# Twelve of sixteen v rows on VectorE in the jobs beside prompt attention

## The chip, the cores and the metric

The kernel runs on one core of one Trainium2 chip. The metric is the device time of one execution in microseconds (us); lower is better. The core has TensorE (PE, matrix products into PSUM), VectorE (DVE), ScalarE (ACT), GpSimd (POOL) and SyncE (SP). Here POOL only issues gathers, SP and ACT issue plain transfers. Each engine runs its own instructions in order and waits on semaphores for the others.

## The reference

One decoder layer for a prompt of 1024 tokens and 8 x 8 sample tokens: RMSNorm with modulation, one input projection into q, k, v, convolution inputs and gates, a short causal convolution, dilated window attention in three head groups, two gated output projections, and then PEER. PEER is what the change touches:

```python
q = (xb @ w_query)...                      # 8 heads, two halves of 128
s1, s2 = q halves @ sub_keys               # 128 scores each, top 16 of each
top_s, top_pos = top_k(v1[:, None] + v2[None, :], 16)
gate = softmax(top_s)
act  = einsum('td,thkd->thk', xb, expert_u[eidx])
coef = gate * gelu(act)
out  = einsum('thk,thkd->td', coef, expert_v[eidx])
```

For each token and head, 16 rows of `expert_u` are dotted with the token's row, and 16 rows of `expert_v` are added up with weights `coef`. Every row is 1024 floats.

## The kernel before

A tile is 128 tokens, and there are 9 of them (the third holds the 64 sample tokens). The first 0.76 ms prepare modulation, the first two tiles and the sample tokens. All else is in `peer`, one program on all engines at once.

**Jobs.** A job is one tile and one head; there are 72, numbered by tile and then head. Loop s (0 to 72) gathers the u rows of job s and the v rows of job s-1. POOL issues them in the order u(s, k), v(s-1, k) for k = 0 to 15. One gather fetches 128 rows, one for each token: 512 KB. The u rows land in a ring of 8 slots, the v rows in another ring of 8. So v row k + 8 can be gathered only once v row k has been used (line 1506 and on: POOL waits on `v_weighed` if TensorE uses row k, on `v_added` if VectorE does).

**The two ways to add a v row.** TensorE: ScalarE writes a diagonal matrix of the weights (line 2107), and `weigh` (line 1787) multiplies it with the row into PSUM. VectorE: `add_row` (line 2459) multiplies and adds the row into `acc`. `on_vector(s, k)` says which engine takes row k of job s. In jobs 0 to 47 VectorE takes the odd rows and TensorE the even ones; from job 48 on VectorE takes 5 rows.

**VectorE's loop.** For each k: a step of the ranking of a later job (`experts`), the dot of u row k (`dot`, line 2443), `add_row` where the v row is its own, then background. At the end of the loop `coefs` (lines 2466 to 2483) makes the weights; line 2483 ends the loop.

**Background.** Beside the jobs runs the front part of the layer for the next three tiles (segments): norm, input projection (line 1682 and others), attention, mixing (line 1700), output projection, queries. `chain_order` numbers its PSUM banks, 6 of which are used in turn. `limit(s, f)` turns the place in the jobs (loop s, fraction f) into the number of the last bank that the background may have reached. VectorE calls `pace.up_to(limit(s, k / 16))` behind every k. TensorE does this behind each of its v rows:

```python
for i, r in enumerate(rows):
    weigh(r)
    pace.up_to(limit(s, min(0.9, (i + 3) / len(rows))))
```

`rows` are TensorE's rows of job s-1. So the number of rows that TensorE has sets where its background goes between them.

**Attention of a segment.** It lies in loops 9 to 12 (first half of the table below) and 33 to 38. There are 12 items (head pair, tile, head) in each segment. For an item TensorE makes scores (mask line 1613, product line 1614) in 2 to 4 banks; VectorE takes their maximum (lines 2236 to 2242, the function `top`); ScalarE the exponentials (line 1948); TensorE transposes them (line 1650); ScalarE copies these to SBUF (line 1967); TensorE multiplies with v (line 1637). The scores of item i+1 stand before the transposes of item i on TensorE, and on ScalarE the exponentials of item i+1 stand before the copies of item i.

Of the kernel before, what the change touches and what calls it, by code (L numbers as in the profile page):

```python
# [1008 lines left out]

JOBS = NT * HEADS  # L1010
WINDOW = 48
LATE = 52
SEG = 3
SEGS_N = NT // SEG
# [10 lines left out]
def width(s):  # L1025
    return TOPK // 2 if s // HEADS == PS else TOPK


def rows_before(s):

    return TOPK * s - TOPK // 2 * min(max(s - PS * HEADS, 0), HEADS)
# [4 lines left out]


def on_vector(s, k):
    return k in ((1, 3, 5, 7, 9, 11, 13, 15) if s < WINDOW else (2, 5, 8, 11, 14))


def added_by():

    on_pe, on_dve = {}, {}
    for s in range(JOBS):
        for k in range(width(s)):
            mine = on_dve if on_vector(s, k) else on_pe
            mine[rows_before(s) + k] = len(mine)
    return on_pe, on_dve
# [131 lines left out]
def peer(nc, io, keep):  # L1181
    with ExitStack() as ctx:
# [161 lines left out]
        def wait_emptied(eng, key):  # L1344
            eng.wait_ge(emptied[number[key] % NB], number[key] // NB + 1)
# [468 lines left out]
        def _(act):  # L1814
# [267 lines left out]
            def raise_h2(t):  # L2082
                act.wait_ge(h2_in[t % 2], 16 * (t // 2 + 1))
                if t == LATE // HEADS:
                    for key in list(number)[-NB:]:
                        wait_emptied(act, key)
                if t > LATE // HEADS + 1:
                    act.wait_ge(u_used, rows_before(HEADS * (t - 1)))
                for c in range(2):
                    act.activation(psB[:, 2 * (t % 2) + c, :], h2[:, t % 2, c * 512:(c + 1) * 512],  # L2090
                                   ACT.Copy).then_inc(h2_raised, 1)
# [35 lines left out]
            for s in range(JOBS + 1):  # L2127
# [19 lines left out]
                if s < JOBS:  # L2147
                    act.wait_ge(gelu_in, s + 1)
                    act.activation(g4[:, 0:width(s)], g3[:, 0:width(s)], ACT.Exp, scale=-GELU).then_inc(gelu_exp, 1)  # L2149
                if s == LATE - 1:  # L2150
                    raise_h2(t)
                if h == 7 and LATE // HEADS < t + 1 < NT:
                    raise_h2(t + 1)
# [6 lines left out]
        def _(dve):  # L2160
# [274 lines left out]
            def dot(s, k):  # L2435
                t, r = s // HEADS, rows_before(s) + k
                if k == 0 and s % HEADS == 0:
                    dve.wait_ge(h2_in[t % 2], 16 * (t // 2 + 1))
                if s >= LATE and (s == LATE or s % HEADS == 0) and k == 0:
                    dve.wait_ge(h2_raised, 2 * (t - LATE // HEADS + 1))  # L2440
                dve.wait_ge(u_in[r % U], 16 * (r // U + 1))
# [80 lines left out]
            for s in range(JOBS + 1):  # L2522
                t, h = divmod(s, HEADS)
                if h == 1 and t:
                    finish(t - 1)
                for k in range(TOPK):
                    if k <= NAMED_AT:
                        next(choosing, None)
                    if k == NAMED_AT:
                        for _ in choosing:  # L2530
                            pass
                        choosing = experts(s + 2) if s + 2 < JOBS else iter(())
                    if TOPK - RANKED <= k:
                        next(choosing, None)
                    if s < JOBS and k < width(s):
                        dot(s, k)
                    if s and k < width(s - 1) and on_vector(s - 1, k):
                        add_row(s - 1, k)
                    pace.up_to(limit(s, k / TOPK))
                if s < JOBS:  # L2540
                    coefs(s)
                if h == 0 and t:
                    gather_up(t - 1)
# [81 lines left out]
```

## Time and profile before

| | |
|---|---|
| time, median of 3 runs | 4194.48 us (4192.9 to 4195.76) |
| profiled execution, its own time | 4189.91 us |
| its span in the profile | 4187.2 us |
| PE / DVE / POOL busy | 78% / 69% / 59% of the span |
| loops 9, 10, 11 (attention of the second segment) | 65, 71, 62 us |
| loops 34, 35, 36, 37 (attention of the third) | 55, 57, 60, 49 us |
| a loop beside other background, 13 | 50 us |

A loop is counted here from one end of `coefs` to the next. "Released by" in the profile names the instruction that ended a wait. POOL's busy time is the time in which it issues gathers; the landing comes later and is given by the view of a line.

### The profile page before, as it was taken

The numbers are of one execution on the slowest core, as the hardware profiler recorded it, in microseconds if no ns is written. First come the engines' busy times: TensorE is split into PE (matmuls) and PEld (weight loads), VectorE is DVE, ScalarE is ACT, GpSimd is POOL, SyncE is SP. The second block draws the span as 40 slices with busy tenths as digits, with TensorE's granted clock in tenths as the row PEclk, the third lists the DMA queues.
The fourth block names the chain that finished last, engine by engine and source line by source line (L and its number), as shares of the span: only waits on it lengthen the run. The fifth ranks groups of instructions, "written<-read, shape, count | busy, mean of one in ns | idle before, by whom it ended". The sixth has DMA issues, their size and how long they took to land. (4 is left out here: it accounts for less than half of the span.)

```text
span 4187.2 us, 33973 instructions
## 1 busy us (share of the span) xinstructions
PE 3280.6 (78%) x9782; PEld 1758.2 (42%) x9798; DVE 2895.2 (69%) x6507; ACT 635.6 (15%) x1759; POOL 2488.9 (59%) x2277
## 2 busy tenths in 40 slices
PE   6978898788888987788888888887777666566666
PEld 1445575654444544455444445444444222222222
DVE  2212111678786777988878987787778788778875
ACT  0020001221012212123110133111111111101010
POOL 0001000477764677567787666876777777777775
PEclk9968898899997899889998898998888888988888
DMA  7316344799997999999999989999999999999998
GB/s 257 124 34 174 98 121 150 277 403 403 393 387 255 331 387 396 352 391 376 401 402 390 385 320 335 390 391 387 387 393 391 373 409 409 408 409 397 405 409 323
DMA packets 578893, 1405.09 MB, mean 336 GB/s; under 512 B 44731, under 2 KB 276347, under 8 KB 578683
## 3 DMA queue, kind: packets, MB, share of 16 engines
q0 software_dynamic: 320080, 1165.57, 71.7%
q1 hardware_dynamic: 223070, 196.45, 15.0%
q10 hardware_dynamic: 35560, 40.91, 2.8%
q8 instruction: 81, 1.33, 0.1%
q14 instruction: 102, 0.84, 0.1%
HBM read 1369.31 MB, written 33.44 MB: 335 GB/s over the span
## 5 line engine op out<-in xcount | busy, mean ns | idle before, releaser
L1787 PE MATMUL peer_psA<-peer_vring,peer_diag 128*128 128x512 f32 x2464 | 1394.8, 706 | 626.4 <-DMA peer_vring<-in_expert_v,peer_idx 474.3
L1501 POOL DMA_INDIRECT peer_uring<-in_expert_u,peer_idx x1088 | 1224.4, 1125 | 713.6 <-DVE peer_idx L2416 360.7
L1511 POOL DMA_INDIRECT peer_vring<-in_expert_v,peer_idx x1088 | 1222.4, 1124 | 548.2 <-issue 301.0
L2443 DVE CUSTOM_DVE_ANT_0 peer_uring<-peer_uring,peer_h 128x1024 f32<-128x1024 f32 x768 | 934.6, 1217 | 218.7 <-DMA peer_uring<-in_expert_u,peer_idx 217.0
L1787 PEld LDWEIGHTS peer_psA<-peer_vring,peer_diag 128*128 128x128 f32 x2464 | 509.6, 221 | 1353.2 <-issue 1165.3
L2459 DVE SCALAR_TENSOR_TENSOR peer_acc<-peer_vring,peer_coef,peer_acc 128x1024 f32<-128x1024 f32 x463 | 593.9, 1283 | 86.2 <-DMA peer_vring<-in_expert_v,peer_idx 80.7
L2443 DVE CUSTOM_DVE_ANT_0 peer_uring<-peer_uring,peer_psB 128x1024 f32<-128x1024 f32 x320 | 388.8, 1215 | 142.8 <-DMA peer_uring<-in_expert_u,peer_idx 142.5
L1682 PE MATMUL peer_psB<-keep_hT,peer_w 128*128 128x384 f32 (+1 forms) x864 | 279.2, 483 | 12.2 <-DMA peer_w<-in_w_in 12.2
L1756 PE MATMUL peer_psB<-peer_w,keep_hT 128*128 128x256 f32 x1152 | 273.4, 393 | 18.4 <-DMA peer_w<-in_w_query 17.3
L1700 PE MATMUL peer_psB<-keep_hT,peer_w 128*128 128x384 f32 (+1 forms) x768 | 250.8, 482 | 20.8 <-DMA peer_w<-in_w_attn_o 20.8
L1756 PEld LDWEIGHTS peer_psB<-peer_w,keep_hT 128*128 128x128 f32 x1152 | 228.5, 200 | 76.5 <-issue 28.2
L2149 ACT ACTIVATE peer_g<-peer_g 128x16 f32<-128x16 f32 (+1 forms) x72 | 15.5, 215 | 1459.7 <-DVE peer_g L2473 1459.7
L1682 PEld LDWEIGHTS peer_psB<-keep_hT,peer_w 128*128 128x128 f32 x864 | 170.4, 198 | 125.8 <-issue 23.9
L1700 PEld LDWEIGHTS peer_psB<-keep_hT,peer_w 128*128 128x128 f32 x768 | 150.4, 197 | 121.4 <-DMA peer_w<-in_w_attn_o 25.0
L2107 ACT ACTIVATE peer_diag<-keep_ident,peer_coef 128x128 f32<-128x128 f32 x616 | 187.8, 388 | 59.8 <-DVE peer_coef L2483 59.8
L1579 PE MATMUL peer_psB<-peer_w,keep_hT 128*128 128x384 f32 x576 | 196.4, 496 | 0.0
L1579 PEld LDWEIGHTS peer_psB<-peer_w,keep_hT 128*128 128x128 f32 x576 | 113.0, 197 | 88.1 <-issue 23.4
L1729 PE MATMUL peer_psB<-peer_w,peer_mT 128*128 128x384 f32 (+3 forms) x432 | 130.6, 461 | 3.0 <-DVE peer_mT L2325 3.0
L1637 PE MATMUL peer_psB<-peer_w,peer_arena 128*128 128x64 f32 x576 | 89.2, 314 | 37.7 <-ACT peer_arena L1967 37.7
L1614 PE MATMUL peer_psB<-peer_w,peer_mT 64*128 64x512 f32 (+3 forms) x224 | 104.9, 552 | 3.4 <-issue 1.8
L1637 PEld LDWEIGHTS peer_psB<-peer_w,peer_arena 128*128 128x128 f32 x576 | 86.3, 232 | 49.1 <-issue 44.6
L1729 PEld LDWEIGHTS peer_psB<-peer_w,peer_mT 128*128 128x128 f32 (+1 forms) x432 | 81.7, 190 | 56.1 <-issue 17.2
(245 smaller groups left out, 2943.8 us busy)
## 6 DMA issues: line engine op xcount, KB each, us to landing
peer_w<-in_w_in SPq DMA_DIRECT2D x102, 512.0 KB, 21.8
peer_w<-in_w_query SPq DMA_DIRECT2D x24, 1024.0 KB, 15.7
peer_w<-in_w_in SPq DMA_DIRECT2D x12, 1536.0 KB, 18.4
peer_uring<-in_expert_u,peer_idx POOLq DMA_INDIRECT x1088, 10.7
peer_vring<-in_expert_v,peer_idx POOLq DMA_INDIRECT x1088, 10.6
front_ring<-in_w_ada POOLq DMA_DIRECT2D x7, 2048.0 KB, 8.3
front_ring<-in_w_ada SPq DMA_DIRECT2D x5, 2048.0 KB, 7.8
peer_w<-in_w_conv_o SPq DMA_DIRECT2D x24, 384.0 KB, 23.1
```

What stands on the lines that cost most here:

```text
L1501: pool.indirect_dma_start(out=uring[:, r % U, :], out_offset=None, in_=io["expert_u"], in_offset=bass.IndirectOffsetOnAxis(ap=idx[:, s % 4 ...
L1511: pool.indirect_dma_start(out=vring[:, r % V, :], out_offset=None, in_=io["expert_v"], in_offset=bass.IndirectOffsetOnAxis(ap=idx[:, s % 4 ...
L1579: last = pe.matmul(dst[:, 0:WQKV], hT[:, k, i * P:(i + 1) * P], wv[:, k, :], start=(k == 0), stop=(k == DC - 1))
L1637: last = pe.matmul(bank(key_o)[:, 0:HD], pT[:, t_slot[g, it, b] % 2, (at % 4) * P:(at % 4 + 1) * P], vv[:, kb, col:col + HD], start=(at == ...
L1682: last = pe.matmul(dst[:, 0:m], wv[:, k, part, :], hT[:, k, 0:m], start=(k == 0), stop=(k == DC - 1))
L1700: last = pe.matmul(dst[:, 0:m], wv[:, KC_AT[q] + k, :], src[:, k, 0:m], start=(k == 0), stop=(k == KC[q] - 1))
L1729: last = pe.matmul(dst[0:R, 0:e - a], mT[:, k, i * P:i * P + R], wv[:, k, :], start=(k == 0), stop=(k == DC - 1))
L1756: last = pe.matmul(dst[:, 0:KD], hT[:, k, j * P:(j + 1) * P], wv[:, k, :], start=(k == 0), stop=(k == DC - 1))
L1787: last = pe.matmul(psA[:, c * 512:(c + 1) * 512], diag[:, a % DG, :], vring[:, r % V, c * 512:(c + 1) * 512], start=first, stop=False, ski ...
L2107: act.activation(diag[:, a % DG, :], ident[:], ACT.Copy, scale=coef[:, s % 4, k:k + 1]).then_inc(diag_set, 1)
L2443: dve.tensor_tensor_reduce(uring[:, r % U, :], uring[:, r % U, :], rows, 1.0, 0.0, ALU.mult, ALU.add, act_[:, k:k + 1]).then_inc(u_used, 1)
L2459: dve.scalar_tensor_tensor(out=acc[:], in0=vring[:, r % V, :], scalar=c, in1=acc[:], op0=ALU.mult, op1=ALU.add).then_inc(v_added, 1)
```

## The change

In jobs 8 to 13 and 32 to 37 VectorE takes 12 of the 16 v rows, and TensorE rows 0, 4, 8 and 12. Their rows are added in loops 9 to 14 and 33 to 38. The counts behind the waits (`on_pe`, `on_dve`) follow from `on_vector`. 48 rows go from TensorE to VectorE; ScalarE writes 48 diagonals fewer.

```diff
+ATTENDING = ((8, 14), (32, 38))
 LATE = 52
...
 def on_vector(s, k):
+    if any(a <= s < b for a, b in ATTENDING):
+        return k not in (0, 4, 8, 12)
     return k in ((1, 3, 5, 7, 9, 11, 13, 15) if s < WINDOW else (2, 5, 8, 11, 14))
```

Line numbers behind it grow by 3. On TensorE, this is what stood in loop 10 from the scores of the seventh item on (psB: the 6 banks; psA: the sum of v rows; the weigh in the middle is v row 6 of job 9, the last one row 8; the program counts 2 products for a weigh, the trace 4):

```order
L1613 MATMUL peer_psB<-keep_mask,keep_identb 128x384
L1614 MATMUL peer_psB<-peer_w,peer_mT 128x384
L1613 MATMUL peer_psB<-keep_mask,keep_identb 128x128
L1614 MATMUL peer_psB<-peer_w,peer_mT 128x128
L1787 MATMUL peer_psA<-peer_vring,peer_diag 128x512 x2
L1613 MATMUL peer_psB<-keep_mask,keep_identb 128x256
L1614 MATMUL peer_psB<-peer_w,peer_mT 128x256
L1613 MATMUL peer_psB<-keep_mask,keep_identb 128x256
L1614 MATMUL peer_psB<-peer_w,peer_mT 128x256
L1650 MATMUL peer_psB<-keep_ident,peer_arena 128x128 x8
L1787 MATMUL peer_psA<-peer_vring,peer_diag 128x512 x2
```

And now at the same place of the same loop:

```order
L1616 MATMUL peer_psB<-keep_mask,keep_identb 128x384
L1617 MATMUL peer_psB<-peer_w,peer_mT 128x384
L1616 MATMUL peer_psB<-keep_mask,keep_identb 128x128
L1617 MATMUL peer_psB<-peer_w,peer_mT 128x128
L1616 MATMUL peer_psB<-keep_mask,keep_identb 128x256
L1617 MATMUL peer_psB<-peer_w,peer_mT 128x256
L1616 MATMUL peer_psB<-keep_mask,keep_identb 128x256
L1617 MATMUL peer_psB<-peer_w,peer_mT 128x256
L1653 MATMUL peer_psB<-keep_ident,peer_arena 128x128 x8
L1790 MATMUL peer_psA<-peer_vring,peer_diag 128x512 x2
```

The weigh between the scores is gone, and the one at the end is now v row 4. Between v row 0 and v row 4 stands all background up to three quarters of the loop (three items, 41 rows of the program) where three weighs stood between. Rows 8 and 12 follow together at 0.9.

On VectorE, rows k = 10 and 11 of the same loop before (dot, add of a v row, ranking, then the maximum of the seventh item's scores):

```order
L2443 ISA peer_uring,peer_act<-peer_uring,peer_h 128x1024
L2443 ISA peer_act 128x1
L2377 TENSOR_TENSOR peer_eq<-peer_v 128x256
L2443 ISA peer_uring,peer_act<-peer_uring,peer_h 128x1024
L2443 ISA peer_act 128x1
L2459 SCALAR_TENSOR_TENSOR peer_acc<-peer_vring,peer_coef,peer_acc 128x1024
L2236 TENSOR_REDUCE peer_mx<-peer_psB 128x1 x2
```

And now:

```order
L2446 ISA peer_uring,peer_act<-peer_uring,peer_h 128x1024
L2446 ISA peer_act 128x1
L2462 SCALAR_TENSOR_TENSOR peer_acc<-peer_vring,peer_coef,peer_acc 128x1024
L2380 TENSOR_TENSOR peer_eq<-peer_v 128x256
L2446 ISA peer_uring,peer_act<-peer_uring,peer_h 128x1024
L2446 ISA peer_act 128x1
L2462 SCALAR_TENSOR_TENSOR peer_acc<-peer_vring,peer_coef,peer_acc 128x1024
L2239 TENSOR_REDUCE peer_mx<-peer_psB 128x1 x2
```

One add more stands behind the dot of k = 10; the maximum stays behind k = 11.

## Rows read from the trace of the kernel before

**Rows 1.** The page's head: the span.

```profile
span 4187.2 us, 33973 instructions
```

**Rows 2.** The page's costliest groups: out<-in, count | busy, mean ns | idle before.

```profile
L1787 PE MATMUL peer_psA<-peer_vring,peer_diag 128*128 128x512 f32 x2464 | 1394.8, 706 | 626.4 <-DMA peer_vring<-in_expert_v,peer_idx 474.3
L2459 DVE SCALAR_TENSOR_TENSOR peer_acc<-peer_vring,peer_coef,peer_acc 128x1024 f32<-128x1024 f32 x463 | 593.9, 1283 | 86.2 <-DMA peer_vring<-in_expert_v,peer_idx 80.7
```

**Rows 3.** Windows of loops: length, PE, PEld, DVE, ACT, POOL busy, granted clock, DMA, GB/s.

```profile
1222.00:1287.00 65.00, 56.87 (x178) 29.53 (x179) 52.21 (x120) 15.47 (x41) 37.19 (x35) 0.89 0.88 319
1287.00:1358.00 71.00, 64.95 (x219) 36.85 (x220) 46.12 (x107) 20.31 (x61) 32.06 (x29) 0.69 0.72 255
1358.00:1420.00 62.00, 53.33 (x195) 29.10 (x198) 47.53 (x115) 18.98 (x58) 35.37 (x33) 0.83 0.80 291
...
1469.00:1519.00 50.00, 43.31 (x114) 22.28 (x113) 41.02 (x92) 7.14 (x17) 40.08 (x33) 0.93 1.05 389
...
2328.00:2382.00 54.00, 45.69 (x125) 22.68 (x124) 49.91 (x113) 7.46 (x17) 35.50 (x33) 0.95 1.04 396
2382.00:2437.00 55.00, 49.04 (x159) 26.91 (x162) 45.89 (x108) 19.17 (x60) 29.88 (x28) 0.74 0.84 318
2437.00:2494.00 57.00, 50.99 (x213) 29.84 (x215) 46.08 (x109) 18.08 (x54) 35.29 (x35) 0.91 0.87 313
2494.00:2554.00 60.00, 50.87 (x198) 30.12 (x200) 45.67 (x104) 14.53 (x44) 38.46 (x35) 0.86 0.97 349
2554.00:2603.00 49.00, 41.33 (x197) 26.05 (x200) 43.20 (x102) 19.69 (x57) 32.54 (x29) 0.90 0.90 323
```

**Rows 4.** Waits in loops 9 to 11: us in total, times, longest.

```profile
POOL peer_vring L1511 <- PE peer_psA L1787: 66.2, 13, 17.1
DVE peer_mx L2236 <- PE peer_psB L1614: 45.3, 24, 5.9
```

**Rows 5.** Waits in loops 34 to 37.

```profile
POOL peer_vring L1511 <- PE peer_psA L1787: 51.5, 16, 14.0
...
DVE peer_mx L2236 <- PE peer_psB L1614: 29.0, 21, 5.4
```

**Rows 6.** TensorE in loop 10: start us, length us, engine, line, op [idle before].

```profile
1295.95 2.07 PE L1614 MATMUL peer_psB<-peer_w,peer_mT 64*128 64x512 f32 x2 [0.36 <-issue]
...
1312.74 0.63 PE L1613 MATMUL peer_psB<-keep_mask,keep_identb 128*128 128x512 bf16 x1
...
1315.31 3.42 PE L1787 MATMUL peer_psA<-peer_vring,peer_diag 128*128 128x512 f32 x4
...
1322.53 1.88 PE L1787 MATMUL peer_psA<-peer_vring,peer_diag 128*128 128x512 f32 x4
...
1330.33 0.53 PE L1613 MATMUL peer_psB<-keep_mask,keep_identb 128*128 128x384 bf16 x1
...
1341.61 3.62 PE L1787 MATMUL peer_psA<-peer_vring,peer_diag 128*128 128x512 f32 x4
```

**Rows 7.** Windows by clock in loop 10, columns as in the windows above.

```profile
1294.30:1318.20 23.90, 21.24 (x58) 12.13 (x59) 15.29 (x36) 4.30 (x12) 6.11 (x6) 0.50 0.54 199
1318.20:1328.50 10.30, 8.79 (x47) 5.32 (x44) 6.99 (x19) 4.04 (x11) 6.96 (x7) 1.00 0.72 234
```

**Rows 8.** VectorE at the end of loop 10: dot of row 13, last of `coefs`.

```profile
1343.72 1.22 DVE L2443 CUSTOM_DVE_ANT_0 peer_uring<-peer_uring,peer_h 128x1024 f32<-128x1024 f32 x1
...
1358.05 0.17 DVE L2483 TENSOR_TENSOR peer_coef<-peer_g,peer_gates 128x16 f32<-128x16 f32 x1
```

**Rows 9.** POOL in loop 10: v row 10, the next u row.

```profile
1319.00 0.94 POOL L1511 DMA_INDIRECT peer_vring<-in_expert_v,peer_idx  x1 [17.05 <-PE peer_psA L1787]
1320.24 0.94 POOL L1501 DMA_INDIRECT peer_uring<-in_expert_u,peer_idx  x1 [0.30 <-issue]
```

**Rows 10.** The line of the u gathers in loops 9 to 11: landing.

```profile
DMA to landing us min/median/max: 5.1/7.3/13.5
```

## The prediction

> **What bounds the kernel now.** I read the head of the page first, for the span [rows 1], then its groups, for what one add costs on either engine [rows 2], then windows cut at the ends of the loops that the change touches [rows 3], then who waits for whom in them [rows 4, 5], and last TensorE, VectorE and POOL in one of these loops, in order of time [rows 6 to 10].
>
> Beside other background a loop is bound by the gathers. In loop 13 the DMA engines are busy throughout (share 1.05) while TensorE has work for 43.3 of 50 us and VectorE for 41.0 [rows 3]. In the seven loops beside attention (9 to 11 and 34 to 37) the DMA share is 0.72 to 0.97, the loops are mostly longer, and something else is the bound: VectorE waits for scores, 45.3 us in three loops and 29.0 us in four, and POOL waits 66.2 and 51.5 us until TensorE has used a v row and freed its slot [rows 4, 5]. So there the engines go round an item together: scores, maximum, exponentials, transposes, products. TensorE holds the largest part of that round, 65.0 of 71 us in loop 10 [rows 3].
>
> VectorE and TensorE pass three quarters of the background of such a loop at about the same time as VectorE passes three quarters of its rows. In loop 10 TensorE reaches that mark at 1341.61, where it weighs v row 8 [rows 6], and VectorE dots u row 13 at 1343.72 [rows 8]. I call it the mark.
>
> **The change part by part.**
>
> *Weighs taken off TensorE.* One takes four products of 706 ns, 1394.8 / 616 = 2.26 us with its overlap [rows 2]; 48 make 108.7 us. Four leave each loop, and three of them (rows 2, 4 and 6, with row 4's now standing where row 8's stood) lie ahead of the mark. At most 3 x 2.26 = 6.8 us a loop, 7 x 6.8 = 47 us in the seven loops, comes off the round. In the other five loops it is worth nothing, since gathers or VectorE end last there.
>
> The lower bound comes from the items of loop 10. From the first scores of one item to those of the next it took 16.8 us (1295.95 to 1312.74) with no weigh in it; 17.6 (to 1330.33) with two weighs of 3.42 and 1.88 us; 18.0 us (to 1348.35, 9 further rows of the same pattern) with two more at about 3.6 us [rows 6]. Two weighs cost an item only about 1 us. The reason is in the clock: the granted share was 0.50, that is 1.2 GHz, from 1294.3 to 1318.2, and 1.00, that is 2.4 GHz, for the 10.3 us from there on [rows 7]. It rose as the weigh at 1315.31 was ending. TensorE was busy for 21.24 of the 23.9 us at the low level, most of it with scores, transposes and products with v, and none of that had brought the clock up. So a weigh in this stage pays for itself by the clock that follows. By this row three weighs fewer give a loop 1.5 to 2 us, 7 x 2 = 14 us in all; loops 35 to 37, now at 0.86 to 0.91 [rows 3], could even lose. I take 30 us, the middle of 14 and 47, since five of the seven loops run nearer to 2.4 GHz than loop 10 does.
>
> The Trainium skill (TensorE: Matmul & The Clock Gate, part 1, "What's actually happening") says that the low clock is the default and that activity of the engine releases it. By that rule alone the long busy stretch at 0.50 should have ended by itself, the clock would stay as it is now, and this term would be the full 47 us; the trace has it end at a weigh, so the row decides against the rule's plain form.
>
> *The gathers run dry.* This is what the change adds without a line for it. POOL gathers v row k + 8 only when row k is used, and u row k + 9 is behind that in its queue. Now TensorE's row k is weighed when the background stands at (k + 4) / 16 of the loop, and row k + 8 is needed at (k + 8) / 16: four rows ahead. The new rows 0, 4, 8, 12 are weighed at 0, 0.75, 0.9 and 0.9. So v row 12 can be asked for only behind the mark, when VectorE is at its own row 12, and u row 13 comes behind it. From the mark to the dot of row 13 this takes a weigh (2.26), POOL's start (0.27 behind the weigh, 1315.31 + 3.42 to 1319.00 [rows 6, 9]), one gather to the next (1.24), and the landing (5.1 at least, 7.3 in the middle [rows 10]): 8.9 to 11.1 us. Now it takes 2.1 us. The delay is 9.0 us by the middle landing. VectorE's three added adds ahead of the mark (3 x 1.283 = 3.8 us [rows 2]) partly fill it, so 5.2 to 9.0 us a loop; where VectorE is late for other reasons, nothing. I take 6, nearer to the lower, since a queue that has drained lands faster than the middle: 7 x 6 = 42 us.
>
> POOL's long waits now do no harm, because four rows of u lie in the ring meanwhile: the 17.05 us wait in loop 10 [rows 9] stands beside a VectorE that waits for scores and not for a row.
>
> *Adds put on VectorE.* 48 x 1.283 = 61.6 us [rows 2], 5.1 us a loop. Ahead of the mark the wait for scores hides them (45.3 / 3 = 15.1 and 29.0 / 4 = 7.3 us a loop [rows 4, 5]). Behind it stands one more add, v row 14, with only row 13's landing before it: 1.28 us a loop, 9 us in seven. Loop 33 has VectorE busy for 49.9 of 54 us [rows 3], and attention begins only in its last fifth; there the 5.1 us have 1 to 4 us of cover at most. I take 4 of 5.1. In loops 12, 13, 14 and 38 the gathers end last, VectorE has some 9 us to spare, as in loop 13 [rows 3], and I take 0, with 5.1 each, 20 us, as the other bound.
>
> *Diagonals off ScalarE.* 48 fewer, off the path; 0, between a gain of 0.4 us a loop and nothing.
>
> Sum: -30 + 42 + 9 + 4 = +25 us. The profiled execution took 4189.91 us, 2.7 us more than its span [rows 1]; the median of the runs is 4194.48, 4.6 us above it. The changed kernel comes to 4189.9 + 25 = 4215 us in such an execution, 4219.5 as a median.
>
> **The rivals.**
>
> *A, VectorE absorbs the work (faster).* TensorE's clock stays as it is, the round shortens by the whole 47 us, and VectorE, later by its added adds, finds row 13 landed. Then each loop lasts as long as VectorE's work. The seven loops have 326.7 us of it now; with 7 x 5.1 added, 7 us of small waits and 4 us a loop of landing they come to 398 against 419 us [rows 3]: 21 us less, and 4 us back in loop 33. Some 17 us faster, 4177 us. For it: the waits of VectorE for scores are real slack. Against it: it holds only if the delay behind the mark stays under 4 us in each loop, and no row shows that much room there.
>
> *B, the terms cancel (same).* The weighs give 47 us and the delay is 5 us a loop: -47 + 35 + 9 + 4 = +1, 4196 us.
>
> *C, nothing hides the adds (slower still).* VectorE becomes the bound in all twelve loops, because its rows 1, 2 and 3 now follow one another and each waits for its own landing: 61.6 us on top, 4256 us. Against it: loop 13's spare time, and the DMA share of 0.72 to 0.97 in the others.
>
> *D, the clock stays at 1.2 GHz between the marks.* The weighs give 14 us and the delay is 9 us a loop: -14 + 63 + 9 + 4 = +62, 4256 us as well. It is the forecast at its upper end.
>
> **How the numbers follow.** The forecast, between +9 and +50 us, gets 0.48, C and D together 0.15, B 0.17, A 0.20. A change of less than 0.2%, 8.4 us, can't be told from none here. Faster than that is A alone, 0.20; within it B, 0.17; slower the rest, 0.63. The likeliest case alone spans 4203 to 4245. The range that should hold the time 8 times in 10 takes in A's price and most of C and D: 4176 to 4252.
>
> **What would show it.** Right: one long wait of POOL for TensorE in each of the seven loops, at v row 12, instead of several; VectorE's wait for u rows in these loops at 4 us or more each, just behind the dot of row 12; its wait for scores shorter; the granted clock in loops 11 and 35 to 37 below 0.83 and 0.86; loop 33 longer by about 4 us; loops 12 to 14 and 38 unchanged. Wrong: the seven windows shorter than 419 us in all, with no wait for u rows; or a clock that rises between the marks without a weigh.

## The result and the profile after

The changed kernel takes 4281.39 us (median of 4 runs, 4279.10 to 4286.09), the kernel before, beside it, 4195.12 us (4192.90 to 4204.19). The ratio is 1.0208, with a 95% interval of 1.0194 to 1.0221: 86 us slower. The forecast was slower by 25 us, with a range up to 4252. The direction was right; the size lies outside the range. Of all executions in this document one stands apart, 6895.11 us among the six of e11_pace_five_eighths; its times and ratio below leave that one out.

The page of the changed kernel, head and the groups that answer to [rows 1, 2]. Lines stand 3 higher than before (weigh L1790, u gather L1504, v gather L1514, dot L2446, add L2462):

```profile
span 4279.6 us, 33590 instructions
...
L1790 PE MATMUL peer_psA<-peer_vring,peer_diag 128*128 128x512 f32 x2272 | 1311.2, 718 | 690.3 <-DMA peer_vring<-in_expert_v,peer_idx 489.5
...
L1514 POOL DMA_INDIRECT peer_vring<-in_expert_v,peer_idx x1088 | 1220.6, 1122 | 646.4 <-PE peer_psA L1790 321.9
L2446 DVE CUSTOM_DVE_ANT_0 peer_uring<-peer_uring,peer_h 128x1024 f32<-128x1024 f32 x768 | 934.5, 1217 | 293.9 <-DMA peer_uring<-in_expert_u,peer_idx 291.8
...
L2462 DVE SCALAR_TENSOR_TENSOR peer_acc<-peer_vring,peer_coef,peer_acc 128x1024 f32<-128x1024 f32 x511 | 655.4, 1283 | 87.7 <-DMA peer_vring<-in_expert_v,peer_idx 80.3
```

48 weighs (192 matmuls in the trace) have gone and 48 adds have come, at nearly the unit prices of before (718 and 706 ns for a weigh's product, 1283 for an add). The work did what the change says; the span grew by 92.4 us elsewhere. Windows cut at the ends of loops 9, 10, 11, 33 and 34 to 37, columns as in [rows 3]:

```profile
1224.00:1297.00 73.00, 52.07 (x163) 28.44 (x163) 57.70 (x125) 14.60 (x38) 30.90 (x30) 0.76 0.69 256
1297.00:1374.00 77.00, 60.71 (x203) 37.85 (x204) 51.29 (x115) 19.14 (x57) 35.55 (x34) 0.61 0.69 253
1374.00:1452.00 78.00, 57.59 (x183) 35.34 (x186) 51.92 (x115) 17.58 (x54) 34.54 (x35) 0.63 0.64 239
2359.00:2418.00 59.00, 41.55 (x110) 20.72 (x109) 54.91 (x117) 6.29 (x14) 33.37 (x32) 0.84 1.02 387
2418.00:2487.00 69.00, 52.57 (x158) 30.82 (x161) 50.07 (x112) 17.99 (x56) 25.97 (x24) 0.60 0.55 205
2487.00:2563.00 76.00, 53.21 (x190) 33.03 (x192) 50.94 (x109) 16.57 (x49) 42.72 (x38) 0.68 0.78 272
2563.00:2632.00 69.00, 51.65 (x176) 31.58 (x178) 49.65 (x108) 13.47 (x40) 34.27 (x32) 0.65 0.74 270
2632.00:2699.00 67.00, 50.06 (x201) 32.27 (x203) 49.13 (x112) 18.65 (x54) 33.70 (x31) 0.70 0.75 270
```

Loop by loop, the seven beside attention went from 419 to 508 us: 89 of the 92.4. Their DMA share fell to 0.55 to 0.78 and the granted clock to 0.60 to 0.76. The waits in loops 9 to 11, and then in 34 to 37, against [rows 4, 5] (total us, times, longest):

```profile
POOL peer_vring L1514 <- PE peer_psA L1790: 96.4, 3, 33.4
...
DVE peer_uring L2446 <- DMA peer_uring<-in_expert_u,peer_idx: 32.3, 6, 13.2
...
DVE peer_mx L2239 <- PE peer_psB L1617: 25.1, 15, 3.5
...
POOL peer_vring L1514 <- PE peer_psA L1790: 108.2, 5, 29.1
DVE peer_uring L2446 <- DMA peer_uring<-in_expert_u,peer_idx: 60.2, 8, 15.8
...
DVE peer_mx L2239 <- PE peer_psB L1617: 13.4, 12, 1.9
```

VectorE's account closes with these. It had waited 4.6 us for u rows in the seven loops and now waits 92.5: 88 us more. It had waited 74.3 us for scores [rows 4, 5] and now waits 38.5: 35.8 us less, which is what its added adds take (28 x 1.283 = 35.9). So its adds took the place of its waits for scores, as forecast, and what is left over, 88 of 89 us, is the wait for u rows.

POOL's 13 waits of three loops have become 3, each over 31 us. One of the stalls in order of time, loop 35 of the changed kernel; first POOL, then VectorE, then TensorE (start, length, engine, line, [idle before]):

```profile
2519.34 1.38 POOL L1504 DMA_INDIRECT peer_uring<-in_expert_u,peer_idx  x1 [0.30 <-issue]
2542.93 0.94 POOL L1514 DMA_INDIRECT peer_vring<-in_expert_v,peer_idx  x1 [22.22 <-PE peer_psA L1790]
2544.18 0.94 POOL L1504 DMA_INDIRECT peer_uring<-in_expert_u,peer_idx  x1 [0.30 <-issue]
...
2531.67 1.20 DVE L2446 CUSTOM_DVE_ANT_0 peer_uring<-peer_uring,peer_h 128x1024 f32<-128x1024 f32 x1
...
2549.50 1.23 DVE L2446 CUSTOM_DVE_ANT_0 peer_uring<-peer_uring,peer_h 128x1024 f32<-128x1024 f32 x1 [15.82 <-DMA peer_uring<-in_expert_u,peer_idx]
...
2555.45 2.08 DVE L2239 TENSOR_REDUCE peer_mx<-peer_psB 128x1 f32<-128x512 f32 x4
...
2539.46 3.20 PE L1790 MATMUL peer_psA<-peer_vring,peer_diag 128*128 128x512 f32 x4
...
2561.36 1.94 PE L1640 MATMUL peer_psB<-peer_w,peer_arena 128*128 128x64 f32 x8 [10.39 <-ACT peer_arena L1970]
```

VectorE dots row 12 at 2531.67. TensorE weighs v row 4 only at 2539.46, 7.8 us later; POOL has waited since 2520.7 and issues v row 12 at 2542.93 and u row 13 at 2544.18; the row lands and is dotted at 2549.50. The maximum of an item (2555.45) stands behind that on VectorE, and TensorE then waits 10.39 us for ScalarE's copies behind it. Windows of the clock in that loop:

```profile
2490.50:2501.00 10.50, 8.26 (x28) 3.45 (x28) 8.69 (x12) 0.31 (x1) 8.53 (x7) 1.00 0.88 313
2501.00:2542.90 41.90, 32.55 (x102) 21.47 (x105) 28.14 (x65) 10.57 (x29) 15.75 (x14) 0.51 0.69 233
2542.90:2555.60 12.70, 8.06 (x30) 3.99 (x29) 5.44 (x8) 0.00 (x0) 9.92 (x10) 1.00 0.83 284
2555.60:2563.00 7.40, 1.64 (x8) 1.67 (x9) 6.77 (x21) 3.37 (x11) 5.80 (x6) 0.50 1.01 387
```

Between v row 0 and v row 4 TensorE runs at 1.2 GHz for nearly all of 41.9 us and is busy for 32.55 of them; the clock rises as the weigh of v row 4 ends.

### The profile page after: what moved, and what is told of

It reads as the page before. It is cut to its first block and busy times, and to the rows that moved or that the text cites. A ratio compares the mean times of both kernels' runs of the same rounds, so it can differ in the third digit from the quotient of the medians.

```text
span 4279.6 us, 33590 instructions
## 1 busy us (share of the span) xinstructions
PE 3258.9 (76%) x9591; PEld 1763.7 (41%) x9606; DVE 2951.6 (69%) x6555; ACT 621.2 (15%) x1711; POOL 2478.5 (58%) x2277
## 3 DMA queue, kind: packets, MB, share of 16 engines
q1 hardware_dynamic: 223070, 196.45, 14.8%
## 5 line engine op out<-in xcount | busy, mean ns | idle before, releaser
L1790 PE MATMUL peer_psA<-peer_vring,peer_diag 128*128 128x512 f32 x2272 | 1311.2, 718 | 690.3 <-DMA peer_vring<-in_expert_v,peer_idx 489.5
L1504 POOL DMA_INDIRECT peer_uring<-in_expert_u,peer_idx x1088 | 1216.0, 1118 | 716.6 <-DVE peer_idx L2419 358.3
L1514 POOL DMA_INDIRECT peer_vring<-in_expert_v,peer_idx x1088 | 1220.6, 1122 | 646.4 <-PE peer_psA L1790 321.9
L2446 DVE CUSTOM_DVE_ANT_0 peer_uring<-peer_uring,peer_h 128x1024 f32<-128x1024 f32 x768 | 934.5, 1217 | 293.9 <-DMA peer_uring<-in_expert_u,peer_idx 291.8
L1790 PEld LDWEIGHTS peer_psA<-peer_vring,peer_diag 128*128 128x128 f32 x2272 | 477.7, 225 | 1380.2 <-issue 1145.2
L2462 DVE SCALAR_TENSOR_TENSOR peer_acc<-peer_vring,peer_coef,peer_acc 128x1024 f32<-128x1024 f32 x511 | 655.4, 1283 | 87.7 <-DMA peer_vring<-in_expert_v,peer_idx 80.3
L2446 DVE CUSTOM_DVE_ANT_0 peer_uring<-peer_uring,peer_psB 128x1024 f32<-128x1024 f32 x320 | 388.9, 1215 | 138.6 <-DMA peer_uring<-in_expert_u,peer_idx 138.4
L2110 ACT ACTIVATE peer_diag<-keep_ident,peer_coef 128x128 f32<-128x128 f32 x568 | 173.8, 388 | 59.6 <-DVE peer_coef L2486 59.6
L1640 PE MATMUL peer_psB<-peer_w,peer_arena 128*128 128x64 f32 x576 | 114.8, 375 | 87.0 <-ACT peer_arena L1970 87.0
L1640 PEld LDWEIGHTS peer_psB<-peer_w,peer_arena 128*128 128x128 f32 x576 | 111.5, 291 | 97.8 <-issue 84.2
L1617 PE MATMUL peer_psB<-peer_w,peer_mT 64*128 64x512 f32 (+3 forms) x224 | 125.7, 651 | 4.3 <-issue 3.6
## 6 DMA issues: line engine op xcount, KB each, us to landing
peer_vring<-in_expert_v,peer_idx POOLq DMA_INDIRECT x1088, 11.1
```

The costliest lines, as they stand in the source:

```text
L1504: pool.indirect_dma_start(out=uring[:, r % U, :], out_offset=None, in_=io["expert_u"], in_offset=bass.IndirectOffsetOnAxis(ap=idx[:, s % 4 ...
L1514: pool.indirect_dma_start(out=vring[:, r % V, :], out_offset=None, in_=io["expert_v"], in_offset=bass.IndirectOffsetOnAxis(ap=idx[:, s % 4 ...
L1640: last = pe.matmul(bank(key_o)[:, 0:HD], pT[:, t_slot[g, it, b] % 2, (at % 4) * P:(at % 4 + 1) * P], vv[:, kb, col:col + HD], start=(at == ...
L1790: last = pe.matmul(psA[:, c * 512:(c + 1) * 512], diag[:, a % DG, :], vring[:, r % V, c * 512:(c + 1) * 512], start=first, stop=False, ski ...
L2110: act.activation(diag[:, a % DG, :], ident[:], ACT.Copy, scale=coef[:, s % 4, k:k + 1]).then_inc(diag_set, 1)
L2446: dve.tensor_tensor_reduce(uring[:, r % U, :], uring[:, r % U, :], rows, 1.0, 0.0, ALU.mult, ALU.add, act_[:, k:k + 1]).then_inc(u_used, 1)
```

## The experiments

Theory 1: POOL's gathers run dry at v row 12, since TensorE frees v row 4's slot at three quarters of the loop. Theory 2: the added adds are not hidden. Theory 3: the clock, without weighs in the middle of a loop, makes the difference. An edit is shown against the changed kernel. All ratios are to the kernel before, run beside it on the same chip; "u" is VectorE's wait for u rows in the seven loops. "Ahead" is how many rows before v row k + 8 is needed TensorE's row k is weighed by its pace, the smallest in the loop.

| run | VectorE's rows | ahead | u, us | seven loops, us | ratio (95%) |
|---|---|---|---|---|---|
| before | 8 | 4 | 4.6 | 419 | 1 |
| after | 12 | 0 | 92.5 | 508 | 1.0208 (1.0194 to 1.0221) |
| e1_pace_quarter | 12 | 8 | 0 | 423 | 0.9972 (0.9955 to 0.9988) |
| e4_pace_half | 12 | 4 | 0 | 428 | 1.0027 (1.0016 to 1.0038) |
| e11_pace_five_eighths | 12 | 2 | 36.8 | 456 | 1.0106 (1.0077 to 1.0135) |
| e3_late_rows | 12 | 6.6 | 0 | 437 | 0.9999 (0.9987 to 1.0012) |
| e2_no_margin | 8 | 0 | 101.0 | 509 | 1.0240 (1.0216 to 1.0263) |
| e6_pace_alone | 8 | 8 | 0 | 413 | 0.9939 (0.9920 to 0.9959) |
| e10_pace_twelve_again (e6 again) | 8 | 8 | 0 | 404 | 0.9947 (0.9930 to 0.9965) |
| e7_weighs_twice | 12 | 8 | 0 | 429 | 0.9990 (0.9977 to 1.0003) |
| e8_pace_all | 8 | 8 | 0 | 422 | 0.9956 (0.9940 to 0.9972) |
| e9_adds_first_half | 12 and 8 | 8 | 0 | 408 | 0.9943 (0.9921 to 0.9965) |
| e5_first_half | 12 and 8 | 8 and 4 | 4.7 | 425 | 0.9971 (0.9957 to 0.9985) |

One execution's loops scatter: e6 and e10 are one kernel, and loop 10 took 70.2 us in the one and 60.5 in the other. Differences of 10 us in a sum of loops say nothing; the ratios decide.

**e1, the pace alone is mended.** TensorE weighs rows 0, 4, 8, 12 at 0, 0.25, 0.5 and 0.75 of the loop:

```diff
-                    pace.up_to(limit(s, min(0.9, (i + 3) / len(rows))))
+                    ahead = (i + 1) / 4 if any(a <= s - 1 < b for a, b in ATTENDING) else (i + 3) / len(rows)
+                    pace.up_to(limit(s, min(0.9, ahead)))
```

> The changed split (12 rows on VectorE), but TensorE's background behind its rows 0, 4, 8, 12 goes to 0.25, 0.5, 0.75, 0.9 of the loop, so row 4 is weighed eight rows before v row 12 needs its slot. Theory 1 (the gathers run dry at v row 12, all else follows): the seven loops beside attention lose their wait for u row 13, median 4175 to 4205 us. Theory 2 (the 48 adds on VectorE are not hidden): no change from the changed kernel, 4270 to 4285. Theory 3 (TensorE's clock, since fewer weighs): clock in loop 11 still below 0.7, 4240 to 4270.

Measured 4185.81 against 4198.38 us: the loss is gone, with all 48 adds still on VectorE. In its trace POOL's longest wait for TensorE in loops 9 to 11 is a quarter of the changed kernel's, and VectorE's waits there hold no row for u at all (the clock in loop 11 is 0.80, not below 0.7 as theory 3 had it):

```profile
POOL peer_vring L1514 <- PE peer_psA L1790: 28.7, 8, 8.1
DVE peer_mx L2240 <- PE peer_psB L1617: 21.5, 16, 2.7
```

**e2, the pace alone is spoilt.** The split of before (8 and 8), but no weigh between the start and three quarters of the loop:

```diff
-        return k not in (0, 4, 8, 12)
+        return k % 2 == 1
...
+                    ahead = (0, 0.75, 0.75, 0.9, 0.9, 0.9, 0.9, 0.9)[i] if any(a <= s - 1 < b for a, b in ATTENDING) else (i + 3) / len(rows)
```

> The split of before (8 rows on either engine), but in the twelve jobs TensorE weighs rows 0 and 2, then takes the background to 0.75, then row 4: the place of row 4 as in the changed kernel, no add moved. Theory 1: nearly all of the loss is here, 4250 to 4290 us, with VectorE waiting 8 to 19 us a loop for u row 13. Theory 2: 4190 to 4200. Theory 3 (clock; eight weighs a loop, but in the middle none): 4225 to 4260 with no wait for u rows.

Measured 4293.56 us, as slow as the changed kernel and slower (3.6 us above theory 1's range), with no add moved and no weigh taken away. Its waits in loops 34 to 37:

```profile
POOL peer_vring L1514 <- PE peer_psA L1790: 117.2, 7, 29.3
DVE peer_uring L2447 <- DMA peer_uring<-in_expert_u,peer_idx: 66.9, 10, 17.7
```

e1 and e2 together settle the main cause: the loss goes with the pace of the weighs and not with the engine that adds. Between the dots of u rows 12 and 13 the seven loops spend 22.4 us in all in the kernel before, 103.7 in the changed kernel, 17.0 in e1 and 108.5 in e2. Theory 2 falls as the main cause. Theory 3 does not fall here: e2 has all weighs (127 us busy in the seven loops, as before), but none in the middle of a loop, and its clock is low too (0.64 to 0.81 by loop).

**e3, other rows.** TensorE takes rows 0, 12, 13, 14 at the changed kernel's pace: the slots that it frees late are wanted only in the next loop.

```diff
-        return k not in (0, 4, 8, 12)
+        return k not in (0, 12, 13, 14)
```

> Twelve rows on VectorE, and TensorE takes rows 0, 12, 13 and 14: the background stands between its first and second weigh just as in the changed kernel, but the slot that v row 12 needs is freed by VectorE's row 4. Theory 1: no wait for u rows, 4180 to 4215 us, although the clock in the loops beside attention stays low. Theory 2: 4270 to 4290. Theory 3: the clock below 0.75 there and 4245 to 4280.

Measured 4197.88 against 4198.38 us, no wait for u rows. The pace is that of the changed kernel; only which v rows hang on it differs. Its loops 9 to 11 and 34 to 37, columns as in [rows 3]:

```profile
1224.90:1427.70 202.80, 169.86 (x549) 100.55 (x553) 159.64 (x349) 50.91 (x145) 111.72 (x102) 0.67 0.84 296
2388.10:2622.50 234.40, 194.85 (x698) 120.27 (x709) 198.41 (x435) 66.44 (x198) 138.96 (x123) 0.69 0.89 321
```

The granted clock is as low as over the same loops of the changed kernel (0.67 and 0.66), and the loss is not there. So theory 3 falls here as the main cause.

**e4 and e11, the dose.** As e1, with `(i + 2) / 4` and with `(i + 2.5) / 4`: v row 4 is weighed at 0.5 and at 0.625.

> As the first run of this call, with 0.5, 0.75, 0.9, 0.9: row 4 is weighed four rows before v row 12 needs its slot, the lead that every row had before the change. Theory 1: like the first run within 10 us, 4175 to 4205 us. Theory 2: 4270 to 4285. Theory 3: 4240 to 4270.

> The changed split, with v row 4 weighed at 0.625 of the background instead of 0.75: two rows ahead of the need, halfway between the changed kernel (none) and the half pace (four). By the traces TensorE reaches its mark about 4.6 us behind VectorE's dot of row 12, and it takes 10.2 us from the start of that weigh to the dot of row 13. Two rows of VectorE's are some 7.5 us of a loop of 60. If this sum holds, VectorE waits 13.2 - 7.5 = 5.7 us a loop for u rows, 40 us in the seven loops instead of 92, and the time lies about halfway between the two: 4230 to 4250. If TensorE is not behind VectorE, as the prediction had it, the 9 us chain less 7.5 leaves under 2 us a loop, and the time is near that of the half pace: 4205 to 4220.

Measured 4205.26 us for e4, 19 us above e1 where 10 at most were expected, and 4231.91 us for e11 (1.0106, or 4239 on the 4194.5 us of the first table). With 4, 2 and 0 rows ahead the wait for u rows is 0, 36.8 and 92.5 us; 40 were expected for e11. Its waits in loops 34 to 37:

```profile
POOL peer_vring L1514 <- PE peer_psA L1790: 76.8, 6, 26.7
...
DVE peer_uring L2447 <- DMA peer_uring<-in_expert_u,peer_idx: 25.4, 7, 8.9
```

That decides between the two readings in e11's text: TensorE reaches its mark behind VectorE, not with it. In e4 loop 14 took 65.2 us instead of some 53. There TensorE, ahead of v row 4, stood 15.34 us at a background product for its weights, POOL waited 21.08 us for the weigh behind it, and VectorE 14.1 us for a u row. So whatever holds TensorE ahead of a weigh holds the gathers behind it too, not attention alone. TensorE and then POOL in that loop:

```profile
1552.20 7.41 PE L1703 MATMUL peer_psB<-keep_hT,peer_w 128*128 128x384 f32 x16 [15.34 <-DMA peer_w<-in_w_attn_o]
1559.45 1.88 PE L1790 MATMUL peer_psA<-peer_vring,peer_diag 128*128 128x512 f32 x4
...
1561.60 0.94 POOL L1514 DMA_INDIRECT peer_vring<-in_expert_v,peer_idx  x1 [21.08 <-PE peer_psA L1790]
```

**e6 and e10, early weighs with no add moved.** The split of before, and `(i + 1) / 8` in the twelve loops. (The text below counts two sixteenths too many on either side: TensorE's row k moves from (k + 4) / 16 to k / 16.)

> No add moves: eight rows on either engine as before, but TensorE weighs its row k when the background stands at (k + 2) / 16 of the loop instead of (k + 4 + 2) / 16. If the earlier weighs alone make the gain of the quarter pace, this takes 4180 to 4188. If the gain needs the weighs off TensorE, the rows of u in the ring already cover POOL's waits and this is within 5 us of before: 4190 to 4200. If weighing earlier holds the scores up, slower than that.

> The run with early weighs in twelve loops and no moved add once more, beside the two others on one chip: 0.9939 of before within 0.002.

Measured 4167.55 against 4196.77 us, and 4175.75 against 4197.06: this is below both ranges expected of e6, beats both kernels and is the best version found, with e9. POOL's waits for TensorE in the seven loops fall from 117.7 to 81.1 us and VectorE's for u rows from 4.6 to 0. Part of the gain comes a loop later: loop 13, whose gathers end last in the kernel before [rows 3], takes 42.7 us in e6 (42.4 in e10) instead of 50, with 28 and not 33 gathers left to it, at the same DMA share:

```profile
1464.10:1506.80 42.70, 40.59 (x115) 21.68 (x115) 39.79 (x89) 6.98 (x16) 34.18 (x28) 1.00 1.05 389
```

**e7, the price of the weighs.** As e1, and every one of TensorE's four rows in the twelve loops is weighed a second time against zeros, so that TensorE has as many weighs as before and VectorE keeps its adds.

```diff
+                    for c in range(2):
+                        last = pe.matmul(psA[:, c * 512:(c + 1) * 512], zeros[:],
+                                         vring[:, r % V, c * 512:(c + 1) * 512], start=False, stop=False,
+                                         skip_group_check=True)
```

> The changed split with the quarter pace, and each of TensorE's four rows in the twelve loops is weighed a second time against a matrix of zeros, so that the sum stays and TensorE has the eight weighs a loop of before, on four rows. If a weigh in these loops pays for itself by the clock that follows it, the seven loops beside attention stay within 10 us of the 423 us of the single weighs, and the run at 4180 to 4196. If a weigh costs its busy time, 48 of them at 2.3 to 3.4 us put 65 to 108 us of work on the bound engine, of which the seven loops show 45 us or more: 4225 and up.

Measured 4189.16 us. Against e1 the ratio rises by 0.0018 (with the two intervals, +-0.0021): 7.5 us, between -1 and 16, for weighs that in the seven loops alone add 44 us of busy time. One window each of e1 and e7, loops 34 to 37:

```profile
2372.20:2606.90 234.70, 195.47 (x720) 118.82 (x730) 198.81 (x436) 66.65 (x198) 142.15 (x126) 0.71 0.88 318
```

```profile
2377.30:2614.90 237.60, 201.69 (x773) 120.68 (x784) 198.95 (x436) 66.66 (x198) 138.94 (x125) 0.82 0.86 312
```

Weighs went from 50.3 to 72.7 us, TensorE's whole busy time only by 6.2: at a granted clock of 0.82 instead of 0.71 the other products took 16 us less. In loops 9 to 11 the whole busy time rose by 10.1 us for 22 us of weighs, at 0.85 instead of 0.77. e7 against e6 has the same number of weighs, 48 adds more: 0.0043 to 0.0051 of the ratio, 18 to 21 us, for 61.6 us of adds.

**e5, e8, e9: how far the pace carries.** e5 is e1 with `ATTENDING = ((8, 14),)`; e8 is the kernel before with `(i + 1) / len(rows)` in all 72 loops; e9 is e5's split with early weighs in all twelve loops.

> The changed split with the quarter pace, in the first six of the twelve loops only (9 to 14); loops 33 to 38 are as in the kernel before. In the run with both halves, loops 9 to 14 came out shorter than before by 13 us and loops 33 to 38 longer by 14 to 15 us in the one profiled execution, and the median was 12.6 us shorter. If the two halves are worth what the loops show, this one is shorter than before by 13 us or more: 4175 to 4186. If the loops of one execution scatter and the gain is spread evenly, half of it stays: 4188 to 4192.

> No add moves, and the pace of the run with eight rows each and early weighs holds in all 72 loops instead of twelve. Where the gathers end last with POOL always busy, an earlier freed slot starts nothing earlier: if so this is within 5 us of that run, some 0.6% below before (4165 to 4176). If the slots hold the gathers up in the other loops too, where POOL waits 240 us for TensorE by the trace of before, it is 20 us or more below that: under 4150.

> Early weighs in all twelve loops (TensorE's row k when the background stands at k / 16), the twelve rows on VectorE only in loops 9 to 14, eight each in 33 to 38. By the loops of the single executions, 9 to 14 take 336 us with twelve rows on VectorE and 340 with eight: then this is 4 us below the run with early weighs and no moved add. If the added adds cost everywhere what they cost over both halves (14 us by the ratios 0.9972 and 0.9939), half of it: 7 us above it.

e5 measured 4187.02 us: its ratio is e1's, and it lies between the two expectations, so it doesn't tell them apart. e8 measured 4179.52, within 5 us of e10 as the first expectation had it (though above its 4176) and not below it: early weighs in the other sixty loops bring nothing that can be seen. e9 measured 4169.37, within the interval of e10: whether the first half gains from moved adds stays open.

## Why the prediction was wrong in size

**What bounds the kernel, and what the change would show: right.** One long wait of POOL in each of the seven loops at v row 12, VectorE's wait for u rows behind the dot of row 12 (7.2 to 15.8 us each, 86.0 of the 92.5; 4 or more were named), shorter waits for scores, clock below 0.83 in loop 11 and below 0.86 in 35 to 37, loop 33 longer by 5.0 us (4 forecast), loops 12, 13, 14 and 38 at 207.5 instead of 203.5 us, within the scatter: all as listed.

**The gathers run dry, +42: the step that failed.** Restoring the four rows of margin under the changed split (e4) takes away 0.0181 of the ratio, 76 us (69 to 83). The chain itself was sized rightly: 8.9 to 11.1 us from the mark to the dot of row 13 were forecast, 10.2 is the mean over seven loops from the start of the weigh of v row 4. (The u row landed in 5.1 to 5.7 us, as the lower end had it; the weigh was longer, 3.20 us in loop 35 against 2.26.) Its start was not. The prediction set TensorE's mark at VectorE's row 12, on the strength of loop 10 [rows 6, 8], and took 3 of 9.0 us off, for VectorE's added adds and a fast landing. The adds did not make VectorE the later of the two, since they took the place of its waits for scores: in the changed kernel the weigh starts 4.6 us behind the dot of row 12 in the mean (5.1, -0.2, 4.3, 6.5, 7.8, 6.5, 2.1). The lag could have been read from the trace before: there the weigh of v row 8 starts 7.5, -0.2, 2.1, 3.9, 4.1, 5.4 and 1.6 us behind the dot of row 12 in the seven loops, 3.5 us in the mean, and loop 10 is the one loop without a lag. TensorE and VectorE in loop 9 of the kernel before:

```profile
1270.01 1.88 PE L1787 MATMUL peer_psA<-peer_vring,peer_diag 128*128 128x512 f32 x4
```

```profile
1262.56 1.21 DVE L2443 CUSTOM_DVE_ANT_0 peer_uring<-peer_uring,peer_h 128x1024 f32<-128x1024 f32 x1
...
1271.21 1.22 DVE L2443 CUSTOM_DVE_ANT_0 peer_uring<-peer_uring,peer_h 128x1024 f32<-128x1024 f32 x1
```

So from the dot of row 12 to that of row 13 a loop takes 4.6 + 10.2 = 14.8 us. Before it took 3.2 in the mean: 8.7 in loop 9, where VectorE waits for scores in between, and 1.9 to 3.5 in the others; the 2.1 that the prediction took off is again loop 10's. The delay is 11.6 us a loop, against 6. Seven times that, 81.3 us, is most of the 89.1 by which the seven loops grew; up to the dot of row 12 they grew by 12.4, behind the dot of row 13 they shrank by 4.6, both no more than single executions scatter by. e11's waits were forecast from the same lag and chain, 40 us, and measured 36.8.

**Weighs off TensorE, -30: mis-sized.** They are worth 7.5 us, between -1 and 16 (e7 against e1, at the quarter pace): the lower bound of 14 or less, and not 30. e7 bears out the lower bound's argument that a weigh in this stage nearly pays for itself by the clock that follows it. Its rows were read too simply. The third item of loop 10 has two banks of scores (1024 columns) and the first two have three (1536), so its 18.0 us can't be set beside their 16.8 and 17.6. And not every weigh was followed by a rise. This is the stretch of loop 10 behind those of [rows 7], and one of its weighs:

```profile
1328.50:1345.50 17.00, 17.00 (x41) 8.98 (x41) 8.24 (x19) 2.95 (x9) 5.23 (x6) 0.50 0.78 278
```

```profile
1333.30 3.78 PE L1787 MATMUL peer_psA<-peer_vring,peer_diag 128*128 128x512 f32 x4
```

The clock stayed at 1.2 GHz behind this weigh and rose only with the next, the one at 1341.61 [rows 6]. The prediction chose a middle value because five loops ran nearer to 2.4 GHz; those lost their clock with their weighs (0.86 to 0.91 in loops 35 to 37 before, 0.63 to 0.79 in e1, where VectorE waits for no u row). In loop 35 of the changed kernel 32.55 us of work in 41.9 us left the clock at 1.2 GHz, and it rose at the weigh behind them. The Trainium skill (TensorE: Matmul & The Clock Gate, "What's actually happening") says that activity releases the low clock; the 32.55 us of work in this row did not, so the row does not bear that sentence out in its plain form.

**The adds, +9 and +4: nearly right in size.** 18 to 21 us by e7 against e6 and e10 (each with some +-10), 13 forecast. Their place is open: the 9 us were put behind the dot of row 13, where the seven loops became no longer. Together with the weighs that is +11 to +14 us for the change without its stall, and e4 measures +11 (7 to 16, some of it perhaps its loop 14); the prediction's terms gave -17. The two errors, 34 us in the stall and 28 in the rest, make up the 62 us between the forecast and the result.

**"POOL's long waits now do no harm": wrong.** e6 and e10 take 36 us or more off them in the seven loops and gain 22 to 26 us. The rows in the ring cover VectorE in the loop itself, but a transfer not started there is made up for later, as in loop 13, where the gathers end last and five fewer were left to e6.

Of the rivals, C and D had the nearest price (4256). C's mechanism fell with e1. D's was there, beyond its price: a long delay (11.6 us a loop, 9 in its sum), a low clock up to the mark and little gain from the weighs (7.5 us, 14 in its sum). The range up to 4252 was meant to take in most of C and D but ends short of their price. What e4's late weights come from, and why e3, without a stall, is 11 us slower than e1, was not tried. (Over the seven loops e3's granted clock is 0.68 in the mean and e1's 0.74; that this is the cause is not shown.)

## What to carry to other kernels

When work is taken from an engine that also frees ring slots, first write down when each slot will now be freed and when its next tenant is needed: here the count of rows set the pace of the frees, and two lines of pacing were worth 99 us (after against e1), while moving the adds, less what the weighs gave back, cost 11 to 14. A lag between two engines is to be read in every loop that the term is multiplied by, since one loop can be the exception. Where a gather queue idles beside a stage that it doesn't bound, freeing its slots earlier can pay in the stage behind it.

## What the runs showed of the hardware

In loop 35 of the changed kernel TensorE stayed at a granted clock of 0.51 through 41.9 us in which it was busy for 32.55, and stood at 1.00 from the end of a weigh (3.20 us) on. In loop 10 of the kernel before it stayed at 0.50 through 17.0 us in which it was busy throughout, with one weigh of 3.78 us inside, and rose with the next weigh. Doubling the weighs with products of zeros raised the granted clock from 0.71 to 0.82 in loops 34 to 37, and their sum went from 234.7 to 237.6 us, within the scatter of single executions; the whole run became 7.5 us longer (-1 to 16): work without any use almost paid for itself. Behind the seven stalls of the changed kernel, where POOL had issued nothing for 22 to 33 us, the first u row landed in 5.1 to 5.7 us, against 7.3 in the middle [rows 10].
